# A decoder layer with a PEER expert FFN: a third token block whose first product goes by gathered rows, dots against a copy of the block in PSUM, and one-hots in one instruction

## The reference, cut to what matters

```python
q = (xt @ w_pq).reshape(T, H, 2, PEER_HALF)
s = einsum('thpd,hpkd->thpk', q, sub_keys)           # 2 x 128 scores a head
s1, i1 = top_k(s[:, :, 0], 16); s2, i2 = top_k(s[:, :, 1], 16)
cand = s1[..., :, None] + s2[..., None, :]           # 256 pairs
top_s, pos = top_k(cand, 16); idx = the pairs' i1 * 128 + i2
g = softmax(top_s)
u = u_tab[ib]                                        # (token, 128, 1024)
a = gelu(einsum('cd,ced->ce', xb, u)) * gb
y = einsum('ce,ced->cd', a, v_tab[ib])
```

## Time and profile before

| | us |
|---|---|
| median of 3 runs | 3114.03 (3112.42 to 3116.7) |
| the profiled execution: its own time, its span | 3114.11, 3112.3 |
| PE, DVE, ACT, POOL busy | 2979.0, 2450.3, 1191.8, 1159.7 |
| PE's weight loads busy | 2686.6 |
| line 1084, z: 2048 matmuls, mean of one | 343 ns |
| line 793, POOL's remainder of u x 128, mean | 2464 ns |
| DMA moved | 695.57 MB |

### The profile page before, as it was taken

The page is one execution under the profiler, slowest core; times in us unless marked ns, Lnnn a source line. Parts: engine busy times, 40 slices in busy tenths (PEclk is TensorE's granted clock), DMA queues, the critical chain, the costliest instruction groups (busy, mean ns, idle before and its releaser), DMA issues. The chain is left out here.

```text
span 3112.3 us, 42565 instructions
## 1 busy us (share of the span) xinstructions
PE 2979.0 (96%) x15866; PEld 2686.6 (86%) x15866; DVE 2450.3 (79%) x4511; ACT 1191.8 (38%) x2213; POOL 1159.7 (37%) x750
## 2 busy tenths in 40 slices
PE   8996998999999999999999999869999999999998
PEld 6886886888999999999999998858888888888887
DVE  4214775455999999999999986569989898999898
ACT  2112332111222466666666656523333333333331
POOL 3222211002656544443444445524434333344331
PEclk9998998999999999999999999989999999999999
DMA  4223222223777666666667677889988888888882
GB/s 172 79 88 132 93 96 82 76 91 114 240 251 255 224 229 239 224 239 243 243 236 240 235 268 280 281 287 314 327 287 307 287 309 307 280 305 297 297 306 78
DMA packets 294024, 695.57 MB, mean 223 GB/s; under 512 B 20432, under 2 KB 136528, under 8 KB 290640
## 3 DMA queue, kind: packets, MB, share of 16 engines
q1 hardware_dynamic: 190928, 316.66, 30.6%
q0 software_dynamic: 73728, 268.47, 25.0%
q10 hardware_dynamic: 29184, 108.01, 9.0%
HBM read 565.13 MB, written 127.93 MB: 223 GB/s over the span
## 5 line engine op out<-in xcount | busy, mean ns | idle before, releaser
L1084 PE MATMUL z_ps<-hT_hi,u_hi 128*128 128x384 f32 x2048 | 703.2, 343 | 18.2 <-POOL u_lo L793 12.7
L1085 PE MATMUL z_ps<-hT_lo,u_hi 128*128 128x384 f32 x2048 | 687.5, 336 | 0.0
L1086 PE MATMUL z_ps<-hT_hi,u_lo 128*128 128x384 f32 x2048 | 687.1, 335 | 0.0
L1393 PE MATMUL y_ps<-v_hi,a_hi 128*128 128x512 f32 x1536 | 600.2, 391 | 24.4 <-DVE y L1521 11.6
L1394 PE MATMUL y_ps<-v_lo,a_hi 128*128 128x512 f32 x1536 | 599.5, 390 | 0.0
L1395 PE MATMUL y_ps<-v_hi,a_lo 128*128 128x512 f32 x1536 | 599.2, 390 | 0.0
L793 POOL TENSOR_TENSOR u_lo<-u_raw,u_hi 128x1024 fp32r<-128x1024 f32 x128 | 315.4, 2464 | 618.2 <-ACT u_hi L789 617.3
L1453 POOL DMA_INDIRECT v_rows<-in_v,room x192 | 286.1, 1490 | 437.8 <-DVE y L1500 414.3
L1084 PEld LDWEIGHTS z_ps<-hT_hi,u_hi 128*128 128x128 f32 x2048 | 387.6, 189 | 20.9 <-POOL u_lo L793 15.3
L1085 PEld LDWEIGHTS z_ps<-hT_lo,u_hi 128*128 128x128 f32 x2048 | 387.6, 189 | 0.0
L1086 PEld LDWEIGHTS z_ps<-hT_hi,u_lo 128*128 128x128 f32 x2048 | 386.6, 189 | 0.0
(11 more groups left out here) (189 smaller groups left out, 4818.7 us busy)
## 6 DMA issues: line engine op xcount, KB each, us to landing
u_raw<-in_uT SPq DMA_DIRECT2D x128, 512.0 KB, 3.7
room<-in_v SPq DMA_DIRECT2D x128, 512.0 KB, 6.3
z<-z_sb ACTq DMA_DIRECT2D x128, 384.0 KB, 5.2
gates<-g_sb ACTq DMA_DIRECT2D x24, 2048.0 KB, 8.8
room<-z SPq DMA_DIRECT2D x16, 1536.0 KB, 9.0
z_in<-z SPq DMA_DIRECT2D x16, 1536.0 KB, 8.2
g_in<-gates SPq DMA_DIRECT2D x16, 1536.0 KB, 17.5
room<-gates SPq DMA_DIRECT2D x15, 1536.0 KB, 17.9
```

The source lines that it names most:

```text
L1084: nc.tensor.matmul(o, u_hi[e][:, k], hT_hi[:, k, cols], start=(k == 0), stop=False)
L1085: nc.tensor.matmul(o, u_hi[e][:, k], hT_lo[:, k, cols], start=False, stop=False)
L1086: last = nc.tensor.matmul(o, u_lo[e][:, k], hT_hi[:, k, cols], start=False, stop=(k == KT - 1))
L1393: nc.tensor.matmul(o, ah, v_hi[p][:, i, c], start=(i == 0), stop=False)
```

## The change

1. Block 2 joins the blocks whose z comes from rows (`UB` = 3), but stays among the six whose v goes by matmuls. z has 5 blocks of columns instead of 6: a tile's halves are 384 and 256 columns. Its second halves share one bank, so PE waits for ACT's copy of the tile before.
2. Block 2's finds and gates are kept (`kept`); its Gelu and product are taken once, on 128 x 128 values in turn 6, and the product instead of the gate is spread by the gate steps of turn 7. `experts_out` takes block 2 without Gelu and product.
3. The dots are 384; `PER_TURN` changes, and the order of blocks is 0, 2, 1.
4. A dot reads h from a copy in PSUM (`h_ps`, two banks); there is one buffer `h_own`, loaded anew for each of the three blocks.
5. `make_hot` is one instruction of 1024 elements.
6. The top-k of block 1 moves to `score`, beside block 0's; ACT makes all copies out of PSUM there. `experts_in` searches two blocks' last head at its start, and has top-k in turns 0 to 5.

```diff
+UB = 3
+ZB = TB - UB
-    PER_TURN = [28, 40, 27, 27, 27, 27, 27, 53]
+    PER_TURN = [24, 46, 36, 36, 36, 36, 84, 86]
+    GATE_BLOCKS = list(range(UB, TB)) + list(range(GB, UB))
+    DOT_BLOCKS = [0] + list(range(GB, UB)) + list(range(1, GB))
...
-        h_own = [sb(f"h_own{b}", [P, D]) for b in range(2)]
-        z_ps = [[bank(f"z_ps{e}{a}") for a in range(2)] for e in range(2)]
+        h_own = sb("h_own", [P, D])
+        kept = sb("kept", [P, 3, PH * TOPK])
+        z_first, z_rest = [bank(f"z_first{e}") for e in range(2)], bank("z_rest")
+        z_ps = [[z_first[e][:, 0:CUT], z_rest[:, e * 2 * P:(e + 1) * 2 * P]] for e in range(2)]
+        h_ps = ctx.enter_context(nc.psum_tensor("h_ps", [P, D], F32))
...
                 def make_hot(step):
-                    for hot, side in ((hot2, 1), (hot1, 0)):
-                        last = nc.vector.tensor_tensor(hot[g][:], bc(iota_ps, 1, 4), bc(iT[:, side, t0:t0 + 4], 2, NK),
-                                                       ALU.is_equal)
+                    nc.vector.tensor_tensor(hot[g][:], bc(bc(iota_ps, 1, 4), 1, 2), bc(iT[:, :, t0:t0 + 4], 3, NK),
+                                            ALU.is_equal).then_inc(hot_in[g], 1)
...
                 def dot(i):
                     if slot == 0:
+                        v.wait_ge(h_here, 16 * (i // (PH * TOPK) + 1))
+                        link(nc.vector.tensor_copy(h_ps[:], h_own[:]))
+                        nc.vector.engine_nop().then_inc(h_taken, 1)
-                    nc.vector.tensor_tensor_reduce(rows_in[r][:], rows_in[r][:], h_own[b][:], 1.0, 0.0, ALU.mult, ALU.add,
+                    nc.vector.tensor_tensor_reduce(rows_in[r][:], rows_in[r][:], h_ps[:], 1.0, 0.0, ALU.mult, ALU.add,
                                                    ahead.z_rows[:, b, slot:slot + 1]).then_inc(row_used, 1)
...
+                        if UB > GB and s == TB - 2 and k == SLOTS - 6:
+                            act.wait_ge(row_used, 2 * PH * TOPK)
+                            nc.scalar.activation(kept[:, 2], ahead.z_rows[:, GB], ACT.Gelu).then_inc(late_gelu, 1)
...
                 def turn(h):
+                    if h:
+                        search(h - 1, 0)
+                    if h < PH - 1:
+                        split_w(h + 1, 0)
+                    if h:
+                        search(h - 1, 1)
+                    if h < PH - 1:
+                        split_w(h + 1, 1)
...
-                        product(r, s)
+                        if s >= SKIP:
+                            product(r, s)
```

More of the change, by code:

```diff
@@ L36 @@
 DT = DB * P
+UB = 3
+ZB = TB - UB
+ZT = ZB * P
 def bc(ap, axis, n):
@@ L895, in turn @@
                     last = isinstance(h, int) and h == PH - 1
-                    query(h, 0)
+                    query(h, 0, 0)
+                    query(h, 0, 1)
                     if not last:
                         split_w(h + 1, 0)
-                    query(h, 1)
-                    scores(h, 0)
+                    query(h, 1, 0)
+                    for a in range(2):
+                        scores(h, 0, a)
+                    query(h, 1, 1)
                     if not last:
@@ L905, in turn @@
                         tiles.hi(0)
[L906 to L911, removed]
+                    for a in range(2):
+                        scores(h, 1, a)
+                    act.wait_ge(s_act, 4 * h + 4)
+                    act.dma_start(d["scores"].rearrange("n h p k -> h p n k")[h][:, 2:TB],
+                                  s_out[:, 2:TB].rearrange("p t a k -> p t (a k)")).then_inc(s_stored, 16)
                 for p in range(2):
@@ L1013, in experts_in @@
         g_stored = [sem(f"g_stored{b}") for b in range(2)]
-        picked_in, h_here = sem("picked_in"), [sem(f"h_own_here{b}") for b in range(2)]
+        picked_in, h_here, h_taken = sem("picked_in"), sem("h_own_here"), sem("h_own_taken")
+        late_gelu = sem("late_gelu")
         row_here = [sem(f"u_row_here{i}") for i in range(RING)]
@@ L1019, in own_rows @@
         def own_rows(s, k):
-            first = 4 if s == 0 else 0
+            first = 6 if s == 0 else 0
             before, n = sum(PER_TURN[:s]), SLOTS - first
@@ L1093, in gates @@
                     for t in range(4):
-                        last = nc.tensor.matmul(g_ps[g][:, t], hot2[g][:, t], hot1_g[g][:, t], start=True, stop=True)
+                        last = nc.tensor.matmul(g_ps[g][:, t], hot[g][:, 1, t], hot1_g[g][:, t], start=True, stop=True)
                     last.then_inc(g_done[g], 1)
@@ L1124, in scale_hot @@
                     for t in range(4):
-                        last = nc.scalar.activation(hot1_g[g][:, t], hot1[g][:, t], ACT.Copy,
+                        last = nc.scalar.activation(hot1_g[g][:, t], hot[g][:, 0, t], ACT.Copy,
                                                     scale=gT[:, t0 + t:t0 + t + 1])
@@ L1149, in _ @@
-                        act.wait_ge(z_done[e], 2 * (2 * m + j) + a + 1)
+                        tile, a = s * SLOTS // 2 + k // 2, k % 2
+                        e, i = tile % 2, tile // 2
+                        if a == 0 and tile < NK - 1:
+                            split_u(tile + 1)
+                        act.wait_ge(z_done[e], 2 * i + a + 1)
                         if a == 0:
-                            wait(act, z_stored[e], 16 * (2 * m + j))
-                        nc.scalar.activation(z_sb[e][:, a * HT:(a + 1) * HT], z_ps[e][a][:, 0:HT],
-                                             ACT.Copy).then_inc(z_read[e], 1)
+                            wait(act, z_stored[e], 16 * i)
@@ L1155, in _ @@
+                        c = slice(0, CUT) if a == 0 else slice(CUT, ZT)
+                        nc.scalar.activation(z_sb[e][:, c], z_ps[e][a], ACT.Copy).then_inc(z_read[e], 1)
                         if a == 1:
[L1156 to L1160 removed]
@@ L1291, in _ @@
                             dot(i)
+                        if UB > GB and s == TB - 2 and k == SLOTS - 2:
+                            v.wait_ge(late_gelu, 1)
+                            link(nc.vector.tensor_tensor(kept[:, 2], kept[:, 2], ahead.picked_g[:, GB], ALU.mult))
+                            nc.vector.engine_nop().then_inc(found_in, 1)
                         if s == TB - 1:
-                            for t in range(DB):
+                            for t in range(ZB):
                                 if PRODUCTS_AT[t] == k:
```

326 lines of the change are left out of this document (168 added, 158 removed).

## The result

| | before | changed |
|---|---|---|
| median, us | 3114.5 (3112.4 to 3116.7, 4 runs) | 3215.2 (3208.0 to 3218.2, 4 runs) |
| ratio, 95% interval | | 1.032 (1.030 to 1.034) |
| span of the profiled execution | 3112.3 | 3214.1 |
| PE, DVE busy | 2979.0, 2450.3 | 2893.8, 2452.0 |
| DMA moved, MB | 695.6 | 744.4 |

What follows compares the result with a forecast made beforehand. PE was taken to bound the kernel, with DVE second. Terms of -27, -40 and +145 us gave +78 on 3114.1, so 3192 us; forecast range 3140 to 3250 (chance 0.45), wider range 3080 to 3290.

Steps and rivals of the forecast that it cites:

- PE: Expert stage: a tile with 256-column second halves takes 7.04 us, a turn 112.6 us, with gates 141.5.
- Dots at 1.22 us with h in PSUM: DVE, expert stage: a dot with its read priced at 1.23 us, bounds 1.21 and 1.65; mean near 1.22 expected.
- Rival 3: Dots on DVE: PSUM does not remove their stretch, 1.65 us each with read; +163 us, 3277 us; chance 0.10.
- One-hots at 1.17: DVE, expert stage: one instruction of 1024 takes 1.17 us (bounds 1.15 and 1.28), 37.5 us a turn instead of 41.
- Score stage: Block 1's top-k moves here, adding 8 us to each DVE turn; PE stays full: nothing, bounds -3 and +10 us.
- Turns 0 and 1: First expert turns: 250 us instead of 277, -27, bounds 225 and 277; DVE's work 238 us, PE's 225.
- Turns 2 to 5: Middle expert turns, DVE the bound: 152 us each plus 5 in turn 2, 613 instead of 653, -40.
- Turns 6 and 7: Late expert turns: three buffers' turnover gives 2.92 us a row, 496 us instead of 351, +145, bounds 407 and 595.
- the engines' floor: DMA in turns 6 and 7: 407 us for 170 rows with every engine busy, 2.4 us a row.
- Last stage: After the expert turns: 31 products and Gelus leave DVE and ACT; nothing gained, bounds -3 and +5 us.
- Rival 1: Late turns: rows keep up at 2.5 us each and the kernel gets faster; -36 us, 3078 us; chance 0.22.
- Rival 2: Late turns: worse turnover, longer landings, lower PE clock, 3.4 us a row; turns 2 to 5 at 157; 3301 us; chance 0.18.

Runs made afterwards that it cites:

- e9_two_hots: The changed kernel with the one-hots again in two instructions of 512 elements instead of one of 1024; 3222.5 us against the changed kernel's 3215.2.

## Why the prediction was right

- *PE.* 256-column halves at 0.12 us: the late turns without rows take 143 and 148 us (141.5 forecast), the first of them with PE busy for 142 of 143. Shown.
- *Dots at 1.22 us with h in PSUM.* Shown: 384 of 384 between 1206 and 1224 ns, and with h in SBUF up to 4.1 us. Rival 3 is out. (Its own term for the late turns, 0.42 us more per three rows, gives 520 us and not the 525 that it adds up; it would have been 3272.)
- *One-hots at 1.17.* They take 1.22: 2 us a turn instead of 3.5.
- *Score stage.* The first copy of z starts at 749.7 us (750.3 before). Nothing, as forecast.
- *Turns 0 and 1.* -12.5 us instead of -27. DVE's work is the 238 us forecast, and without gathers the turns take 252, near my 250; the rows cost turn 1 10 us and turn 0 two, which I had named for turn 1 and not priced.
- *Turns 2 to 5.* -14 us instead of -40: 160 a turn, not 152. This term was mis-sized most, by 26 us. Without rows the four turns take 621 us, where I had 613: 6 of the 8 are turn 2, which I put at 157 and which takes 163. The other 18 are the gathers, 7 in each of turns 3 to 5 less 3 in turn 2. The "some waits for rows" of the forecast had been to cover them.
- *Turns 6 and 7.* +122 us instead of +145: 2.78 us a row instead of 2.92. The mechanism, three buffers in turnover above the engines' floor, is shown from both sides: a fourth buffer takes 63 us off these turns, no rows 182. The size was off with the landing, 6.0 us (in `e9_two_hots`) and not 6.5. About half of this is the issue, with which a landing begins: its mean was 1.19 us in turn 7 before and is 0.94 in the late turns now. That the engines' floor was 407 us is not borne out: with four buffers all that the engines did in the two turns took 377 us of their time (0.91 and 0.93 of 409), some 2.2 us a row; the 1.58 us for a row was the mean of the whole stage, and the late turns had 1.48.
- *Last stage.* +6.5 us to the end, beyond the forecast's 5. The last dot starts at 2136 us, 14 us behind the last copy of z (5 before); DVE's first piece for the stage stands behind it in DVE's queue, and PE waits from 2122 on, where before (second line) it waited 11.0 us:

```profile
PE y_ps L1443 <- DVE a_lo L1564: 19.7, 1, 19.7
PE y_ps L1393 <- DVE a_lo L1513: 11.0, 1, 11.0
```

  The runs agree: from the end of the last copy of z to the end of the kernel are 1080 us where the last dot starts at most some 3 us behind that copy (the late dots without rows, two blocks even, the kernel before spread), 1084 to 1086 at 5 to 9 (before, four buffers, four buffers spread) and 1092 at 14.

The sum is -12.5 - 14 + 122 + 6.5 = +102. The forecast was 24 us short of it, and that it was no more is in part luck: the early turns and the last stage cost 47 us more than forecast, the late turns 23 less.

Rival 1 has its decision at 2.46 us a row if the early turns win the forecast 67 us. With four buffers they win 45, which moves it to 2.33; the rows come at 2.41, and the kernel is 13 us slower than before. With the rows spread it cannot be told from before (0.9994). Rival 2 came true in part. Its sign, turns 2 to 5 over 157 us, is there (160), by the gathers. PE's clock fell to 0.86 in the late turns; with the rows gone it is 1.00, so it follows the waits, and what it adds to them was not measured by itself. The landings did not lengthen (6.0 us, 6.5 before), and the pace was 2.78 us a row, not 3.4. Of the signs of the forecast, the two late turns of about 500 us were 473, with PE busy for 72% and not 60%, since its work took longer at the lower clock.

The part that lost was the third block. The other parts gave 19 us; with an even spread 37, and the spread without them gives 31.

## What to carry to other kernels

Work moved from a full engine to gathered rows is priced by the turnover of its buffers, (issue + landing + use) / buffers, and by the DMA engines' time for a row, and not by the instruction that uses the row; take the larger, and count what else DMA has to do in that stretch. Here the turnover had the mechanism right and its size within 5% (2.92 us forecast, 2.78 measured); the landing under load came from the trace of the kernel before. Deal such rows evenly over the time before buying anything else: here one line of numbers was worth 31 us, and the new code without its third block some 6 more, a difference that the intervals hardly show.

An operand in PSUM frees a dot from POOL's subtraction beside it (1.22 us, against 2.11 in the mean), but that is worth something only where DVE or POOL is waited for: 95 us in one version of this kernel, 2 in another.

## What was not expected of the hardware

- In the late turns the 16 DMA engines took 1.55 us of their time for a gathered block of 512 KB with three buffers and 1.48 with four; with the rows spread it was 1.53 and 1.44. With 36 rows a turn, three or four buffers made no difference (1.45). Whether the number of gathers in flight is the cause was not tested further. The prediction's floor of 2.4 us a row was no floor: with four buffers 2.36 was reached in turn 6 at a share of 0.91.
- A dot of 1024 elements has a median of 1.22 us whether its second operand is in SBUF (1.226) or PSUM (1.221); only with both operands in SBUF did POOL's subtraction stretch it, to 4.1 us at most.
- PE in a turn of which it is idle for 28% was granted 0.86 of its clock in the mean, which is the lower of two levels (1.2 and 2.4 GHz) for 28% of the time, and its 142 us of work took 171.
